# Gate and branch products with tokens on the partitions: two blocks of a transformer on one Trainium2 core

## The reference, cut to what matters

```python
# layer, twice (h is the normed input, 256 x 1024)
y = sigmoid(ga) * (hm @ w_branch_m) + sigmoid(gb) * (ha @ w_branch_a)   # ga, gb = h @ w_in[...]; all 256 x 1024
x = x + y @ w_out
x = x + square(relu(norm(x) @ w_up)) @ w_down
# second block
y = sigmoid(gate_a) * (moba @ w_out_moba) + sigmoid(gate_b) * (stick @ w_out_sb)  # inner width 512 each
x = x + y @ w_mix_out
x = x + peer_ffn(norm(x))     # per token 8 heads x 16 experts, gathered from a table of 16384
```

## Time and profile before

| | |
|---|---|
| median of 3 runs | 1728.43 us (1728.03 to 1728.88) |
| profiled execution | 1727.61 us, span 1725.9 us |
| PE busy | 1602.0 us, 93% |
| DVE, ACT busy | 1170.1 us (68%), 861.8 us (50%) |
| the two layers | to about 847 us |
| second block up to the gathers | about 847 to 1064 us |
| gathers of experts | about 1064 to 1716 us, 421 GB/s |

### The profile page before, as it was taken

How to read it: one execution, slowest core, us unless ns; L and a number is a source line. 1 busy time by engine, 2 the same in 40 slices (tenths; PEclk the granted TensorE clock), 3 DMA queues, 4 the chain that set the end, 5 groups by cost and what they waited for, 6 DMA issues and landing times.

```text
span 1725.9 us, 21298 instructions
## 1 busy us (share of the span) xinstructions
PE 1602.0 (93%) x8116; PEld 1173.5 (68%) x8116; DVE 1170.1 (68%) x2053; ACT 861.8 (50%) x1565; POOL 357.6 (21%) x381
## 2 busy tenths in 40 slices
PE   9999999999999999999999999999988777787876
PEld 7988998888998899888889997555422222222322
DVE  6758766666775876666665557987676677766644
ACT  5556544444465654434465545655444444444443
POOL 0200000000020000000060102545643444444330
PEclk9999999999999999999999999999999999999999
DMA  8443554555544455555534368999999999999996
GB/s 314 170 147 126 198 189 174 192 194 185 189 161 149 143 193 186 195 187 183 191 147 147 147 220 312 403 421 421 421 422 421 421 422 421 422 421 422 421 421 259
DMA packets 67512, 464.97 MB, mean 269 GB/s; under 512 B 7497, under 2 KB 9681, under 8 KB 12242
## 3 DMA queue, kind: packets, MB, share of 16 engines
q0 software_dynamic: 36864, 268.45, 37.5%
q1 hardware_dynamic: 30256, 194.83, 31.3%
q10 hardware_dynamic: 290, 0.33, 0.1%
HBM read 462.53 MB, written 1.06 MB: 269 GB/s over the span
## 4 chain that ended last, share of the span: by engine, by line
PE 63%; DMA 21%; DVE 7%; issue 5%; ACT 2%; POOL 2%; POOLq 0%; ACTq 0%
PE acc L622 13%; PE acc L624 13%; PE acc L623 13%; DMA arena<-in_peer_uv,arena 10%; PE att L647 5%; DMA row_xb<-in_peer_uv,arena 5%; PE acc L647 3%; PE acc L1791 3%; PE att L648 3%; PE acc L1794 2%; DMA row_w_hi<-in_peer_uv,arena 2%; DMA row_w_lo<-in_peer_uv,arena 2%; DMA row_xa<-in_peer_uv,arena 2%; PE acc L648 1%; DVE w_lo L584 1%
## 5 line engine op out<-in xcount | busy, mean ns | idle before, releaser
L584 DVE TENSOR_TENSOR w_lo<-arena,w_hi 128x2048 fp32r<-128x2048 f32 x170 | 388.2, 2293 | 158.7 <-ACT w_hi L577 158.3
L577 ACT CAST w_hi<-arena 128x2048 fp32r<-128x2048 f32 x174 | 331.7, 1908 | 119.0 <-PE acc L624 98.7
L1933 ACT ACTIVATE arena<-arena,small 128x1 f32<-128x1 f32 x256 | 75.4, 294 | 284.7 <-DVE arena L2297 132.0
L2297 DVE SCALAR_TENSOR_TENSOR arena<-arena 128x1024 f32<-128x1024 f32 x122 | 149.2, 1224 | 85.7 <-DMA arena<-in_peer_uv,arena 84.1
L622 PE MATMUL acc<-xa,w_hi 128*128 128x256 f32 x672 | 192.0, 286 | 0.4 <-DVE w_lo L584 0.4
L623 PE MATMUL acc<-xa,w_lo 128*128 128x256 f32 x672 | 190.1, 283 | 0.0
L624 PE MATMUL acc<-xa,w_hi 128*128 128x256 f32 x672 | 190.0, 283 | 0.0
L1791 PE MATMUL acc<-arena,gate_raw 128*128 128x512 f32 x244 | 135.7, 638 | 51.7 <-ACT gate_raw L1943 48.0
L2521 POOL DMA_INDIRECT arena<-in_peer_uv,arena x122 | 134.1, 1099 | 173.4 <-PE acc L1794 133.9
L647 PE MATMUL att<-xa,w_hi 128*128 128x512 f32 x384 | 136.0, 398 | 0.0
L622 PE MATMUL acc<-w_hi,xb 128*128 128x512 f32 (+1 forms) x336 | 130.3, 388 | 2.3 <-DVE xb L768 1.8
(11 more groups left out here) (345 smaller groups left out, 3481.9 us busy)
## 6 DMA issues: line engine op xcount, KB each, us to landing
arena<-in_units SPq DMA_DIRECT2D x174, 1024.0 KB, 4.8
arena<-in_units SPq DMA_DIRECT2D x4, 512.0 KB, 5.2
arena<-in_bias SPq DMA_DIRECT2D x1, 2048.0 KB, 9.8
arena<-in_peer_uv,arena POOLq DMA_INDIRECT x122
x_res<-in_x SPq DMA_DIRECT2D x2, 512.0 KB, 5.8
arena<-m_parked SPq DMA_DIRECT2D x2, 512.0 KB, 3.8
arena<-in_norm_mlp_g SPq DMA_DIRECT2D x2, 512.0 KB, 6.7
arena<-in_norm_g SPq DMA_DIRECT2D x2, 512.0 KB, 5.7
```

The source lines that it names most:

```text
L577: nc.scalar.copy(w_hi[:, s, :], raw[HOME[g]]).then_inc(S["hi_ready"], 1)
L584: nc.vector.tensor_tensor(w_lo[:, s, :], raw[HOME[g]], w_hi[:, s, :].bitcast(F32), ALU.subtract).then_inc(S["lo_ready"], 1)
L2297: nc.vector.scalar_tensor_tensor(row, row, 1.0, hn[:, n // SLOTS, :], ALU.mult, ALU.mult, accum_out=dots[:, n:n + 1]).then_inc(S["rows_use ...
```

## The change

All units of ga, gb, bm, ba, ga2, gb2 and yab become T units. A gate or a branch then comes in pairs of units, 512 columns for all 256 tokens, with tokens on the partitions. DVE copies the layers' gates out of the banks (two copies a pair, in place of one adding reduction a unit) and multiplies, adds per tile of tokens. The sum now has tokens on the partitions, so TensorE transposes it for the output product (`y_pe`, four transposes of 128 x 128 for each column half and tile of tokens), ACT rounds it out of PSUM (`y_act`) and DVE takes the rest (`y_dve`). In yab, even units are now the first branch and odd ones the second.

```diff
-    u += [("ga", i, "F") for i in range(4)] + [("gb", i, "F") for i in range(4)]
-    u += [("bm", i, "F") for i in range(4)] + [("ba", i, "F") for i in range(4)]
+    u += [("ga", i, "T") for i in range(4)] + [("gb", i, "T") for i in range(4)]
+    u += [("bm", i, "T") for i in range(4)] + [("ba", i, "T") for i in range(4)]
...
-    u += [("ga2", i, "F") for i in range(4)] + [("gb2", i, "F") for i in range(4)]
-    u += [("yab", i, "Y") for i in range(4)]
+    u += [("ga2", i, "T") for i in range(4)] + [("gb2", i, "T") for i in range(4)]
+    u += [("yab", i, "T") for i in range(4)]
...
-        def unit_t(banks, s, xh, xl, k0, first, last, key, between=lambda: None):
+        def unit_t(banks, s, xh, xl, k0, first, last, key, between=lambda: None, ahead=lambda t: None, turned=lambda k: None, half_key=None):
             for t in range(TT):
                 if t == 1:
                     between()
-                m = half_t(banks, s, xh, xl, t, k0, first, last)
+                ahead(t)
+                for k in range(4):
+                    if t == 0:
+                        turned(k0 + k)
+                    m = half_t(banks, s, xh, xl, t, k0, first, last, range(k, k + 1))
+                if t == 0 and half_key is not None:
+                    m.then_inc(S["tile_done"], mark("tile_done", half_key))
             m.then_inc(S["unit_done"], mark("unit_done", key))
+        def y_pe(pe, b, t):
+            pe.wait_ge(S["y_ready"], at("y_ready", (b, t)))
+            for k in range(4 * b, 4 * b + 4):
+                m = nc.tensor.transpose(att[2 * t + b][:, (k % 4) * P:(k % 4 + 1) * P], ga[:, t, k * P:(k + 1) * P], ident[:])
+            m.then_inc(S["turned"], mark("turned", ("y", t, b)))
...   # TensorE, layer (the same in the second block with yab 2, mix 0, mix 1)
+            def ahead(name, i, t):
+                if (name, i) == ("ba", 2):
+                    y_pe(pe, 0, t)
+                elif (name, i) == ("wo", 0):
+                    y_pe(pe, 1, t)
+                    pe.wait_ge(S["y_lo"], at("y_lo", (0, t)))
+                elif (name, i) == ("wo", 1):
+                    pe.wait_ge(S["y_lo"], at("y_lo", (1, t)))
...   # half_key: ba 1 and ba 3 only, no unit of yab
+                               ("ba", i) if name == "ba" and i % 2 == 1 else None)
...
             def turn_keys():
+                pe.wait_ge(S["y_lo"], at("y_lo", (1, 1)))
                 pe.wait_ge(S["keys_loaded"], at("keys_loaded", HP - 1))
...   # DVE, layer
+                elif name in ("bm", "ba") and i % 2 == 1:
+                    for t in range(TT):
+                        piece = (ga if name == "bm" else gb)[:, t, cols]
+                        if name == "ba" and t == 0:
+                            dve.wait_ge(S["tile_done"], at("tile_done", (name, i)))
+                        else:
+                            unit(name, i)
+                        nc.vector.tensor_tensor(piece, b[t][:], piece, ALU.mult).then_inc(
...
+                        if name == "ba":
+                            nc.vector.tensor_tensor(y, y, piece, ALU.add).then_inc(S["y_ready"], mark("y_ready", (i // 2, t)))
...   # ACT and DVE, both blocks ("yab", 2 and "mix", 0 in the second)
+                half = {("ba", 2): 0, ("wo", 0): 1}.get((name, i))
+                if half is not None:
+                    y_act(act, xb_hi, half, 0)
                 if 0 < u < NU - 2 and (name, i) not in (("wo", 3), ("up", 0)) and u + 2 not in SPLIT_EARLY:
                     split_hi(act, u + 2)
+                if half is not None:
+                    y_act(act, xb_hi, half, 1)
```

More of the change, by code:

```diff
@@ L1000, in layer_pe @@
                     else:
-                        unit_t(b, s, xh, xl, 4 * (i % 2), i % 2 == 0, i % 2 == 1, ("u", u), between)
+                        unit_t(b, s, xh, xl, 4 * (i % 2), i % 2 == 0, i % 2 == 1, ("u", u), between, lambda t: ahead(name, i, t),
+                               (lambda k: turned_in(name, k)) if name in ("bm", "ba") and i < 2 else lambda k: None,
+                               ("ba", i) if name == "ba" and i % 2 == 1 else None)
                 if (name, i) in TURNED_WITHIN:
@@ L1474, in layer_dve @@
                     decay()
+                half = {("ba", 2): 0, ("wo", 0): 1}.get((name, i))
+                if half is not None:
+                    y_dve(dve, xb_hi, xb_lo, half, 0)
                 if 0 < u < NU - 2 and (name, i) not in (("wo", 3), ("up", 0)) and u + 2 not in SPLIT_EARLY:
                     split_lo(dve, u + 2)
+                if half is not None:
+                    y_dve(dve, xb_hi, xb_lo, half, 1)
                 if (name, i) == ("up", 2):
@@ L1605, in build @@
         for i in range(4):
-            BANKS["ga2", i] = BANKS["gb2", i] = [acc[i]]
+            BANKS["ga2", i] = BANKS["gb2", i] = acc[2 * (i // 2):2 * (i // 2) + 2]
             BANKS["yab", i] = acc[2 * (i % 2):2 * (i % 2) + 2]
@@ L1612, in build @@
                    ("kb", 0): [("qa", 1)], ("kb", 1): [("ka", 1)], ("vb", 0): [("qb", 0), ("qb", 1)],
[2 rows of a table removed]
[2 rows of a table added]
                    ("yab", 2): [("yab", 0)], ("yab", 3): [("yab", 1)], ("mix", 0): [("yab", 2)], ("mix", 2): [("yab", 3)],
                    ("pq", 0): [("mix", 0)], ("pq", 1): [("mix", 1)]}
-        for i in range(4):
-            BEFORE2["gb2", i] = [("ga2", i)]
         for i in range(2, 8):
@@ L1961, in take @@
                         nc.scalar.copy(v[:, t, :], b[t][:]).then_inc(S["emptied_act"], mark("emptied_act", (name, t)))
-                elif name in ("ga2", "gb2"):
+                elif name in ("ga2", "gb2") and i % 2 == 1:
                     unit(name, i)
                     g = ga if name == "ga2" else gb
-                    nc.scalar.activation(g[:, 2 * i:2 * i + 2, :], two, ACT.Sigmoid).then_inc(
-                        S["emptied_act"], mark("emptied_act", (name, i)))
-                elif name == "yab":
-                    act.wait_ge(S["y_ready"], at("y_ready", i))
-                    nc.scalar.copy(xa_hi[:, 2 * i:2 * i + 2, :], ga[:, 2 * i:2 * i + 2, :]).then_inc(S["y_hi"], mark("y_hi", i))
+                    for t in range(TT):
+                        nc.scalar.activation(g[:, t, 512 * (i // 2):512 * (i // 2 + 1)], b[t][:], ACT.Sigmoid).then_inc(
+                            S["emptied_act"], mark("emptied_act", (name, i - 1 + t)))
                 elif name == "pq":
@@ L2008, in second_act @@
                 fresh, late = scored_at(u), scored_at(u - 2)
+                half = {("yab", 2): 0, ("mix", 0): 1}.get((name, i))
+                if half is not None:
+                    y_act(act, xa_hi, half, 0)
                 if 0 < u and (name, i) != ("mix", 3):
                     split_hi(act, u + 2)
+                if half is not None:
+                    y_act(act, xa_hi, half, 1)
                 if late:
@@ L2402, in second_dve @@
                     normalise(scored_at(u - 1)[1])
+                half = {("yab", 2): 0, ("mix", 0): 1}.get((name, i))
+                if half is not None:
+                    y_dve(dve, xa_hi, xa_lo, half, 0)
                 if 0 < u and (name, i) != ("mix", 3):
                     split_lo(dve, u + 2)
+                if half is not None:
+                    y_dve(dve, xa_hi, xa_lo, half, 1)
                 take(name, i)
```

143 lines of the change are left out of this document (65 added, 78 removed), and 6 rows, old and new, of tables (BEFORE, BEFORE2).

## The result

The changed kernel takes 1730.34 us, the median of 22 runs (1729.55 to 1733.83); the kernel before, on the same chip, 1728.26 us (1727.35 to 1729.96, 22 runs). The ratio is 1.0013 with a 95% interval of 1.0007 to 1.0019: 2.1 us slower, clear of the noise of the runs and under the 0.2% from which on a difference counts here. The forecast was 1729.9 us. The profiled execution of the changed kernel has a span of 1729.0 us; that of before has 1725.9.

What follows compares the result with a forecast made beforehand. TensorE's queue was taken to bound the stage before the gathers, DMA bytes the gathers. Layers -0.4 and second block +1.9 gave +1.5 us on the profiled 1727.61; against the median, 1729.9 us, range 1725.4 to 1734.0.

Steps and rivals of the forecast that it cites:

- The layers: Each of two layers: units -2.25 and -0.4, transposes +1.76, waits +0.70, together -0.19 us; -0.4 us for both.
- gb 2 and 3: Last two gate units of a layer, with hm's transposes: 12.7 us in place of 13.13, a gain of 0.4 us.
- The branches up to wo 0's transposes: Units bm and ba: T units -2.25 us, +0.44 a group of four transposes; waits at ba 2 and wo 0, +0.70 a layer.
- The gates of the layers, in which width was given nothing: Units ga 0 to gb 1: DVE's chain behind the scores fixes the end, so the apparent 1.0 us gain counts as nothing.
- the first rival: All six waits hidden (-4.8) and ga windows following TensorE (-2.0): 1723.1 us; waits alone, 1725.1 us; chance 0.11.
- The second block: Gates ga2 and gb2 -2.1, yab units -1.2, transposes +1.76, two waits of 1.72 us +3.44: together +1.9 us.
- Which part of a wait is the signal's: In the layers, `tile_done` at half a unit does not help, since the lo part is late: 0.35 us a wait with restart.
- The keys' new wait: Behind mix 0, the keys' transposes wait for the sum's last rest: free, 8.1 us for TensorE against 7.7 for DVE.
- The first gather: First gather of experts, behind TensorE's queue: starts 1.5 us later than before, with the gather stage's length unchanged.
- Width does give something: Denies the rival that 24 fewer matmuls a unit save no time, losing 8.6 us: 1738.5 us; chance 0.02.
- The sum was not as late in the layers as in yab: Denies the rival that the layers' four sites each wait 1.37 us more, +5.5 us: 1735.4 us; chance 0.17.
- The clock did not fall at the waits: Denies the rival that TensorE drops to 1.2 GHz for a unit at two yab sites, 5.5 us each: 1740.9 us; chance 0.03.

Runs made afterwards that it cites:

- Experiment 6: The change in the two layers alone, second block as before: 1728.86 us with yab's weights packed as in the changed kernel, 1728.15 us packed as before.
- Experiment 3: Changed kernel, with VectorE copying the banks of mo 1, mo 3, ga 1 and ga 3 after the softmax's normalising: 1727.45 us.
- experiment 5: Changed kernel, with each 512-column matmul of the gate and branch units made two of 256 columns: 1739.21 us.
- Experiment 1: Changed kernel, with yab 1 and yab 3 signalling VectorE when their first token tile is done: 1728.61 us.
- experiment 2: Changed kernel with the early signal in yab, and y's transposes in the middle of each token tile's matmuls instead of ahead of them: 1726.42 us.
- experiment 4: Changed kernel with early yab signal, y's transposes in mid-tile, and bank copies behind the normalising, all together: 1723.40 us.
- 11: Fastest kernel (all edits and the new order of two steps), with each 512-column gate and branch matmul made two of 256: 1734.06 us.
- three edits and a new order of two steps: Kernel of experiment 4, with yab 3's products and sums ahead of mix 1's low half, and y's last rest ahead of mix 2's: 1721.52 us.
- experiment 7: Kernel before the change, with the banks of mo 1, mo 3, ga 1 and ga 3 taken after the normalising: 1758.97 us.
- experiment 10: Fastest kernel (all edits and the new order of two steps), with each of y's 48 transposes done twice into the same place: 1726.60 us.

## Why the prediction was right

**The sum.** Expected +1.5 us, measured +2.1. The mechanism stands, not the sum alone: in the stretches the layers cancel (+0.1 us for both, where -0.4 was forecast), and the second block loses 2.0 us (+1.9 forecast). Experiment 6 agrees within its 1.6 us.

**The layers.** Predicted -0.19 each, measured -0.03 and +0.12. ga 0 to gb 1 worth nothing: measured +0.02. gb 2 and 3: 12.7 predicted, 12.71 measured, with some luck: the forecast's terms, 2 x 5.48 and 16 x 0.104, make 12.62, no row shows the 0.104, and the remainder it was set beside gives 0.116. Measured it is 0.109 a transpose. The branches up to wo 0's transposes: -2.25 + 0.88 + 0.67 = -0.70 predicted, -0.57 measured. Behind them two more groups and a restart, +0.91, measured +0.94. The waits were 0.3 us each, as worked out.

**The gates of the layers, in which width was given nothing.** This step rested on one reading: VectorE's chain has the same length behind mo's units and ga's. It is the one that the first rival and an engineer who counts matmuls would get wrong by 1 us and more. Experiment 3 shows it from the other side: with the copies out of that chain, the windows shrink by 0.53 us each; and experiment 5 from a third: units longer by 0.55 us a window lengthen it by 0.13. The forecast's 1.78 us for the transposes was 1.74 in the changed kernel.

**The second block.** Gates -2.1 predicted, -2.24 measured, in windows of 13.71 us where 13.7 was forecast. yab to the keys: -1.2 + 1.76 + 3.44 = +4.0 predicted, +4.26 measured; the two waits 1.72 each predicted, 1.6 recorded. Experiment 1 takes 2.5 of the recorded 3.2 us away by an earlier signal, experiment 2 all but 0.3 by other work ahead. The keys' new wait was forecast free with 0.4 us to spare, and it is (VectorE's last rest ends at 1041.53, the transposes start at 1041.97); when the transposes moved half a tile back, it appeared with 0.8 us. A spare of 0.4 us is a term, not a nothing.

**Which part of a wait is the signal's.** "That `tile_done` comes at half of the unit does not help, since the lo part is what is late": true of the layers, where the lo part starts at 221.11 and the product follows at 223.31 without idle time. In yab the lo part stands at the same distance from the unit's start and leaves the same 0.3 to 0.4 us of wait, which experiment 1 shows; the late signal is the other 1.2 of the 1.6 us. When the weights of mix 0 landed late, the lo part alone made a wait of 1.5 us (experiment 4).

**The first gather** was forecast 1.5 us later and came 2.7 later; 0.5 of this lies in unchanged code, in the first 11 us of the execution, where the change has no part, and 0.6 is what the sum was short by.

**The rivals.** Width does give something (experiments 5 and 11). The sum was not as late in the layers as in yab: 0.3 us. The clock did not fall at the waits of 1.6 us; the stretches with them have 1.00. But the mechanism exists in this kernel, at twice the wait: see below. The stretch that the prediction held against it has 3.6 us of idle time in two pieces of 1.8 us; it could not speak for one of 3.4. The first rival's world, all waits hidden, was forecast at 1725.1 us with the waits alone; the kernel of experiment 2 has 1726.4, with 1.1 us of waits left.

## What to carry to other kernels

Fewer and wider matmuls are worth what the stage lets through. Against narrow ones of the same layout they gave 8.9 us in the changed kernel, and 12.5 once the waits were gone. Yet the changed kernel is 2.1 us slower than the kernel before, since transposes, two late signals and another engine's chain took back what width gave; with three edits and a new order of two steps it is 6.7 us faster. Ask of each stretch whose length it has before you price the engine that became faster; then ask what else the new layout allows (here, banks that come free later), since the gain may need a second edit that was not possible before. When a consumer stands at the head of a queue, signal by half units, or put its wait behind work that is ready.

## What the runs showed of the hardware

A wait can cost more than its length. In experiment 7, TensorE stood still for 3.4 us, and in the next 3.21 us its granted clock was 0.57, near the lower of its two levels (1.2 and 2.4 GHz), so that a wide pair of matmuls took 0.64 us (starts at 164.51 and 165.15) in place of 0.36; a wait of 3.4 us cost 4.9. Waits of 1.6 us, with four transposes behind them, left it at 1.00 (12.81 us from 1009.10 on in the changed kernel).

The Trainium skill says that transposes do not count as busy for the clock in the way that matmuls do (TensorE: Matmul & The Clock Gate, "Part 4: PE-mode transpose"). No run here shows a fall from transposes: in experiment 10, with those of y doubled, the granted clock is 1.00 from 1010 to 1040 us. The longest group of them there, the keys', takes 1.97 us, so this says nothing of longer ones.

A transpose of 128 by 128 in float32 is recorded with 0.27 us and costs 0.11 of TensorE's time between matmuls (experiment 10).
